# In-projection of a hybrid GLA/MLA layer: norm weights and roots applied behind the transposes, first weight loads asked for at once

## The chip, the cores and the metric

One core of one Trainium2 chip. The metric is the device time of one execution in microseconds, as the median of several runs. The profile's span is the time from the first to the last instruction of one profiled execution.

## What is computed

The kernel computes one encoder layer for 1,024 tokens of width 1,024 in float32. Only the head of the layer is touched:

```python
def _rmsnorm(x, g):
    y = x * lax.rsqrt(jnp.mean(x * x, axis=-1, keepdims=True) + EPS)
    return y * g

h = _rmsnorm(x, attn_norm)                  # (1024 tokens, 1024)
z = h @ w_in                                # (1024, 1968)
zq, zk, zv, zgate, zg, zcq, zckv, zkpe = jnp.split(z, split_pts, axis=-1)
...
gate_logit = zgate @ w_gate_up + b_gate     # decays of the gated linear attention
o_gla = _rmsnorm(gla_chunked(zq, zk, zv, ...), gla_out_norm) * silu(zg)
q  = _rmsnorm(zcq, q_a_norm) @ w_uq         # latent attention: head norms, rotary, softmax
kv = _rmsnorm(zckv, kv_a_norm) @ w_ukv
...
x = x + concat([o_gla, o_mla]) @ w_out
h = _rmsnorm(x, mlp_norm)
x = x + square(relu(h @ w_up)) @ w_down
```

The root of a token's mean square is one factor for a row of `h`, and the norm weight is one factor for a column of `h`. So `z = root(token) * ((x * weight) @ w_in)`.

## The kernel before

**Products in two parts.** A float32 product is made as three products of rounded operands: a "high" part is a rounded copy that ACT writes, a "low" part is the rest, which DVE or POOL subtracts, and `split_product` (L1741 in `mm`) adds high*high, high*low and low*high in PSUM. Every operand tile therefore passes through ACT and then DVE or POOL before TensorE can use it.

**The in-projection.** The 1,024 tokens are 8 blocks `b` of 128. The columns of `w_in` are four groups `q`: q = 0 is the 416 columns of the MLA latents together with 16 gate columns (432, `ZM`), q = 1 to 3 are 512 columns each (V, G, and Q with K). `in_project(q, b)` makes one tile of 128 tokens by one group: 8 depth tiles `k`, three products each, 24 products into PSUM bank `(8q + b) % 4`. In group q = 0 each block of x is also prepared. The order before is: ACT squares the block (`square_x`, L876), POOL makes the root (`x_rstd`, L681 and L682), DVE multiplies the block with the root and the broadcast norm weight `gain` (`norm_x`, L1214), TensorE transposes it in two halves of four (`norm_T`, L1756), ACT writes the high part (`norm_hi`, L850), DVE the low part (`norm_lo`, L1225).

**The weights.** SP loads one depth tile of weights at a time into a ring of four buffers (`raw`, `piece`, L456). For q = 0 the 16 gate columns come with a second small load for each tile (L461). A ring buffer is free when the low part that was made of it is done (`wlo_done`). ACT makes the high part (`in_high_part`), DVE the low part for q = 0 (`first_low_part`, L1342) and POOL for q >= 1 (`in_low_part`, L693). High and low parts have 10 slices: tiles 0 and 1 of the next group fit beside the 8 of the current one, and tiles 2 to 7 wait until the last block's products have freed a slice. In SP's queue, tiles 0 to 5 of q = 1 come first, then `m_uq` and `m_ukv` (the MLA up-projections), then tiles 6 and 7.

**Order within an engine.** Each engine works through a list written out by hand. POOL's list at the start is: gain load, identity, roots of blocks 0 to 7 with four small loads among them, constants (`causal`, `freq`, `ones`), four loads (`gqk` twice, `gn`, `wgate`), and then, for each block of each group, the low parts of the next group at b = 0 (tiles 0 and 1) and b = 7 (tiles 2 to 7), and the roots of the MLA latents (`c_rs`) at step `START[b] - 1`, the first at s = 5. DVE scales the latents with that root in step s = 6 (`LATENTS`), and TensorE transposes them at the end of step s = 7 (`LATENTS_T`, L1827), before the first product of q = 1.

**After the first tile of q = 1** DVE copies it out (`tile_out(8)`, L1262) and then runs `rotary_angles`. ACT waits for the angles, makes sine and cosine, and then copies the first heads out of PSUM; TensorE waits for these copies in step s = 9.

## Time and profile before

| | |
|---|---|
| median of 3 runs | 1200.38 us (1198.56 to 1200.74) |
| the profiled execution | 1200.04 us |
| its span | 1198.3 us |
| mean granted TensorE clock | 0.991 |
| busy: PE, DVE, ACT, POOL | 1160.1, 780.2, 473.7, 481.4 us |
| DMA | 158.41 MB, mean 132 GB/s |

The profiled execution lasts 1.7 us longer than its span; the rest is start and end around the first and last instruction. Times within the profile are microseconds from the span's start. In a timeline, each row gives the start and the duration; rows of several instructions of the same kind are merged, with their count. A note in brackets tells how long the engine had been idle and what released it.

### The profile page before, as it was taken

To read this page: it belongs to the slowest core of one execution; us is meant where nothing else is said; L and a number is where in the kernel's file an instruction comes from. 1 tells how busy PE (TensorE), PEld (TensorE's weight loads), DVE (VectorE), ACT (ScalarE), POOL (GpSimd) and SP (SyncE) were. 2 spreads that over 40 slices of the span, in tenths; PEclk is the share of its full clock that TensorE was granted. 3 is DMA by queue.
4 is the path that set the end of the run, shared out by engine and by line. 5 is a ranking of instruction groups with operands and counts; after the bars stand their busy time and mean duration, and the time that the engine had idled before them with its cause. 6 is when DMAs were issued, how large, how long until landed. Compare 5 with 4: busy or idle time off the path is not lost.

```text
span 1198.3 us, 15216 instructions
## 1 busy us (share of the span) xinstructions
PE 1160.1 (97%) x5586; PEld 944.4 (79%) x5586; DVE 780.2 (65%) x1012; ACT 473.7 (40%) x907; POOL 481.4 (40%) x365
## 2 busy tenths in 40 slices
PE   6999999989999999999999999999998999999998
PEld 5967677768878788887788888888876888888887
DVE  5454866535656665137668557865787888888963
ACT  5344534215545555125612233323424334443441
POOL 2442545210000114305844444445435556555652
PEclk9999999999999999999999999999998999999999
DMA  7331342264111103421354342331559785356642
GB/s 239 90 98 62 109 121 87 71 180 172 27 28 43 38 1 114 151 88 71 93 171 141 134 147 94 125 126 62 202 179 357 263 282 192 113 186 210 212 123 88
DMA packets 97353, 158.41 MB, mean 132 GB/s; under 512 B 9024, under 2 KB 38736, under 8 KB 97280
## 3 DMA queue, kind: packets, MB, share of 16 engines
q1 hardware_dynamic: 95728, 152.53, 38.6%
q10 hardware_dynamic: 1008, 3.67, 0.8%
q0 software_dynamic: 544, 1.24, 0.5%
q8 instruction: 45, 0.74, 0.3%
q14 instruction: 28, 0.23, 0.1%
HBM read 115.46 MB, written 41.94 MB: 131 GB/s over the span
## 4 chain that ended last, share of the span: by engine, by line
PE 84%; DVE 8%; issue 3%; ACT 2%; DMA 2%; POOL 1%; SPq 1%; ACTq 0%; DVEq 0%; POOLq 0%
PE ps L1741 79%; PE ps L1961 3%; DVE t_all L1515 1%; DVE g_cum L1305 1%; DVE t_new L1515 1%; PE ps L1756 1%; PE ps L1813 1%; DVE dr_lo L1515 1%; POOL wi_lo L693 1%; DMA gain<-in_attn_norm_dram 1%; DMA up_raw<-in_w_up_dram 1%; DMA r_raw<-in_w_down_dram 1%; ACT q_stage L850 0%; PE ps L1898 0%; DVE a_lo L1515 0%
## 5 line engine op out<-in xcount | busy, mean ns | idle before, releaser
L1741 PE MATMUL ps<-dr_hi,dl_hi 128*128 128x512 f32 x448 | 175.5, 392 | 4.1 <-DVE dr_lo L1515 4.1
L1741 PE MATMUL ps<-dr_hi,dl_lo 128*128 128x512 f32 x448 | 175.3, 391 | 0.0
L1741 PE MATMUL ps<-dr_lo,dl_hi 128*128 128x512 f32 x448 | 175.3, 391 | 0.0
L814 POOL TENSOR_TENSOR ua_lo<-up_raw,ua_hi 128x1024 fp32r<-128x1024 f32 x46 | 116.7, 2539 | 118.1 <-ACT ua_hi L850 118.1
L836 POOL TENSOR_TENSOR dl_lo<-l_raw,dl_hi 128x512 fp32r<-128x512 f32 x64 | 101.6, 1613 | 74.5 <-ACT dl_hi L850 74.0
L1741 PE MATMUL ps<-wi_hi,a_hi 128*128 128x512 f32 (+1 forms) x256 | 105.1, 411 | 3.5 <-POOL wi_lo L693 2.1
L1741 PEld LDWEIGHTS ps<-dr_hi,dl_hi 128*128 128x128 f32 x448 | 84.8, 189 | 22.9 <-issue 3.3
L1741 PE MATMUL ps<-a_hi,ua_hi 128*128 128x512 f32 x256 | 99.9, 390 | 2.0 <-ACT u_two L850 1.8
L836 POOL TENSOR_TENSOR dl_lo<-s_all,dl_hi 128x512 fp32r<-128x512 f32 x48 | 74.7, 1574 | 63.5 <-ACT dl_hi L850 62.6
L1741 PE MATMUL ps<-a_hi,ua_lo 128*128 128x512 f32 x256 | 99.6, 389 | 0.0
L1741 PE MATMUL ps<-a_lo,ua_hi 128*128 128x512 f32 x256 | 99.6, 389 | 0.0
L1741 PE MATMUL ps<-wi_hi,a_lo 128*128 128x512 f32 (+1 forms) x256 | 99.3, 388 | 0.0
L1741 PE MATMUL ps<-wi_lo,a_hi 128*128 128x512 f32 (+1 forms) x256 | 99.2, 388 | 0.0
L1741 PEld LDWEIGHTS ps<-dr_lo,dl_hi 128*128 128x128 f32 x448 | 84.7, 189 | 17.7
L1741 PEld LDWEIGHTS ps<-dr_hi,dl_lo 128*128 128x128 f32 x448 | 84.7, 189 | 17.6
L850 ACT ACTIVATE ua_hi<-up_raw 128x1024 fp32r<-128x1024 f32 x48 | 50.5, 1057 | 87.1 <-PE ps L1741 78.7
L1515 DVE TENSOR_TENSOR dr_lo<-r_raw,dr_hi 128x512 fp32r<-128x512 f32 x64 | 72.5, 1132 | 16.8 <-ACT dr_hi L850 16.7
L1741 PE MATMUL ps<-m_kT,m_qT 96*128 96x512 f32 (+3 forms) x192 | 77.2, 512 | 4.0 <-ACT m_p L1040 4.0
L1741 PE MATMUL ps<-tx_hi,ua_hi 128*128 128x512 f32 x192 | 75.5, 393 | 2.3 <-DVE u_three L1515 2.3
L1741 PE MATMUL ps<-tx_lo,ua_hi 128*128 128x512 f32 x192 | 75.4, 393 | 0.0
L1741 PE MATMUL ps<-tx_hi,ua_lo 128*128 128x512 f32 x192 | 75.2, 392 | 0.0
L850 ACT ACTIVATE dl_hi<-l_raw 128x512 fp32r<-128x512 f32 x64 | 39.8, 622 | 85.3 <-PE ps L1741 83.9
(221 smaller groups left out, 2470.7 us busy)
## 6 DMA issues: line engine op xcount, KB each, us to landing
r_raw<-in_w_down_dram SPq DMA_DIRECT2D x144, 256.0 KB, 3.5
hidden<-stage SPq DMA_DIRECT2D x72, 256.0 KB, 2.0
up_raw<-in_w_up_dram SPq DMA_DIRECT2D x16, 1024.0 KB, 5.6
l_raw<-hidden SPq DMA_DIRECT2D x64, 256.0 KB, 3.4
raw<-in_w_in_dram SPq DMA_DIRECT2D x24, 256.0 KB, 3.0
z_gla<-z_stage SPq DMA_DIRECT2D x16, 256.0 KB, 2.1
raw<-in_w_out_dram SPq DMA_DIRECT2D x16, 256.0 KB, 5.9
xs<-in_x_dram SPq DMA_DIRECT2D x8, 512.0 KB, 8.7
```

The costliest lines, as they stand in the source:

```text
L693: pool.tensor_tensor(wi_lo[:, n % SLICES, 0:width], raw[:, k % RING, 0:width], wi_hi[:, n % SLICES, 0:width].bitcast(F32), ALU.subtract).t ...
L814: pool.tensor_tensor(ua_lo[n % UP_RING][:, :, :], up_source(g, product), ua_hi[n % UP_RING][:, :, :].bitcast(F32), ALU.subtract).then_inc( ...
L836: pool.tensor_tensor(slot(dl_lo, t), left_source(t), slot(dl_hi, t).bitcast(F32), ALU.subtract).then_inc(dllo_done, 1)
L850: return act.activation(dst, src, ACT.Copy, scale=scale)
L1305: last = dve.tensor_tensor_scan(g_cum[:, t, blk], ones[:, :], g_log[:, t, blk], 0.0, ALU.mult, ALU.add)
L1515: return dve.tensor_tensor(out_, in0, in1, op)
L1741: return pe.matmul(dst, lhsT, rhs, start=start, stop=stop, skip_group_check=onto)
L1756: last = pe.transpose(bank4(4 + j)[:, i, :], src[:, (4 * j + i) * P:(4 * j + i + 1) * P], ident[:, :])
L1813: last = pe.transpose(bank4(4 + i // 4, DQK)[:, i % 4, :], m_qk[:, b % 2, i, :], ident[:, :])
L1961: last = pe.transpose(bank4(4 + c // 4)[:, c % 4, :], m_p[:, i % 2, c * P:(c + 1) * P], ident[:, :])
```

## The change

Blocks of x are transposed as they come from memory. The norm weight is loaded as eight rows of 128 (`gain_row`), transposed on TensorE, and copied to a column for each depth tile (`gain_col`). ACT's high part and DVE's low part of the transposed x are now made for each depth tile apart, with that column as factor, so four instructions of 128 columns stand in the place of one of 512. The root of the token is applied where a result tile is copied out of PSUM: copies become products with `rstd`; for the G group it goes into the scale of the tanh and the factor 0.5 (`half_rstd`).

For q = 0 all eight weight tiles have buffers (`raw_late` for tiles 4 to 7), and the 16 gate columns of all tiles come in one load (`raw_gate`). SP asks for the gain rows, block 0, the gate columns, the eight tiles and blocks 1 to 7 without waiting; ACT no longer issues loads of x. ACT squares block b + 1 after it has made that block's high parts, where it used to square block b + 2 before the high parts of block b + 1. TensorE multiplies the identity with itself nine times around the first transposes (`warm_up`). The first block's products start when half of its depth tiles are there. The load of the MLP's norm weight moves from POOL to SP. POOL's wait for the eight normed blocks ahead of its four loads goes.

```diff
 # SP
+            sp.dma_start(gain_row[:, :], attn_norm[0].rearrange("(k p) -> k p", p=P)).then_inc(gain_in, 16)
             sp.dma_start(x0[:, 0, :], x_d[0]).then_inc(x_in[0], 16)
+            sp.dma_start(raw_gate[:, :, :], w_in_d[:, :, C_GATE:C_GATE + GR].rearrange("k p n -> p k n")).then_inc(raw_in[0], 16)
             for k in range(KT):
                 in_piece(0, k)
+            for b in range(1, NB):
+                sp.dma_start(x0[:, b, :], x_d[b]).then_inc(x_in[b], 16)
...
+            sp.wait_ge(omT_ready, MH)
+            sp.dma_start(gain[:, :], mlp_norm[0].partition_broadcast(P)).then_inc(gain_in, 16)
 # POOL
-            pool.dma_start(gain[:, :], attn_norm[0].partition_broadcast(P)).then_inc(gain_in, 16)
...
-            pool.wait_ge(xn_ready, NB)
             pool.dma_start(gqk[:, 0, :], q_head_norm[0].partition_broadcast(P)).then_inc(phase_in, 16)
...
-            pool.wait_ge(omT_ready, MH)
-            pool.dma_start(gain[:, :], mlp_norm[0].partition_broadcast(P)).then_inc(gain_in, 16)
 # ACT
+            def x_hi(b, j):
+
+                act.wait_ge(xT_ready, 2 * b + j + 1)
+                for i in range(4):
+                    k = 4 * j + i
+                    last = copy(a_block(a_hi, k, b), bank4(4 + j)[:, i, :], gain_col[:, k:k + 1])
+                last.then_inc(ahi_done, 1)
...
+            act.wait_ge(const_ready, IDENT)
+            copy(m_rden[:, 0:1], ident[:, 0:1])
+            act.wait_ge(gain_ready, 1)
+            x_hi(0, 0)
+            act.wait_ge(raw_in[0], 32)
+            copy(wi_hi[:, 0:KT, MLA_W:ZM], raw_gate[:, :, :])
+            for k in range(2):
+                in_high_part(0, k)
+            x_hi(0, 1)
+            for k in range(2, KT):
+                in_high_part(0, k)
             x_square(0)
...
             for b in range(NB):
-                if b + 4 < NB:
-                    x_load(b + 4)
-                if b + 2 < NB:
-                    x_square(b + 2)
                 if b + 1 < NB:
-                    norm_hi(0, b + 1)
+                    for j in range(2):
+                        x_hi(b + 1, j)
+                    x_square(b + 1)
 # DVE
-            def norm_lo(r, b):
...
+            def x_lo(b, j):
+                dve.wait_ge(ahi_done, 2 * b + j + 1)
+                for i in range(4):
+                    k = 4 * j + i
+                    last = stt(a_block(a_lo, k, b), bank4(4 + j)[:, i, :], gain_col[:, k:k + 1],
+                               a_block(a_hi, k, b).bitcast(F32), ALU.mult, ALU.subtract)
+                last.then_inc(alo_done, 1)
...
                 if q == 0:
-                    dve.tensor_copy(zm[:, b, :], tile[:, 0:ZM]).then_inc(z_out, 1)
+                    dve.wait_ge(rstd_ready, b + 1)
+                    dve.tensor_scalar(zm[:, b, :], tile[:, 0:ZM], root, None, ALU.mult).then_inc(z_out, 1)
                 elif q == 1:
-                    dve.tensor_copy(z_stage[:, n % 2, :], tile).then_inc(z_out, 1)
+                    if b == 0:
+                        dve.tensor_scalar(half_rstd[:, :], rstd[:, 0, :], 0.5, None, ALU.mult)
+                    dve.tensor_scalar(z_stage[:, n % 2, :], tile, root, None, ALU.mult).then_inc(z_out, 1)
...
 # TensorE
+            def warm_up(n):
+
+                for _ in range(n):
+                    mm(ps[:, 2, 0:P], ident[:, :], ident[:, :], True, True)
...
                 for k in range(KT):
+                    if n == 0 and k % 4 == 0:
+                        pe.wait_ge(alo_done, k // 4 + 1)
...
+            pe.wait_ge(const_ready, IDENT)
+            warm_up(3)
+            pe.wait_ge(gain_in, 16)
+            pe.transpose(ps[:, 3, 0:KT], gain_row[:, :], ident[0:KT, 0:KT]).then_inc(gainT_ready, 1)
+            warm_up(2)
+            x_T(0)
+            warm_up(4)
             for b in range(NB):
                 if 1 <= b < NB - 1:
-                    norm_T(0, b + 1, x0[:, b + 1, :])
-                pe.wait_ge(alo_done, 2 * b + 2)
-                in_project(0, b, (lambda: norm_T(0, 1, x0[:, 1, :])) if b == 0 else None)
+                    x_T(b + 1)
+                if b:
+                    pe.wait_ge(alo_done, 2 * b + 2)
+                in_project(0, b, (lambda: x_T(1)) if b == 0 else None)
```

## Rows read from the trace of the kernel before

**Rows 1.** The profile's page, part 1: TensorE busy, share of the span, instructions.

```profile
PE 1160.1 (97%) x5586; PEld 944.4 (79%) x5586; DVE 780.2 (65%) x1012; ACT 473.7 (40%) x907; POOL 481.4 (40%) x365
```

**Rows 2.** Chain in order of time, 0 to 230 us: start, us, what.

```profile
1.29 6.86 DMA gain<-in_attn_norm_dram
...
9.61 1.95 PE ps L1756 x8
...
12.96 4.69 PE ps L1741 x12
...
19.30 2.35 PE ps L1741 x12
```

**Rows 3.** Timeline, all engines, start of the span: start us, us, engine, line, operation.

```profile
0.80 0.39 SPq L467 DMA_DIRECT2D x<-in_x_dram  x1
...
22.28 0.44 PE L1741 MATMUL ps<-wi_hi,a_hi 128*128 128x432 f32 x1
```

**Rows 4.** Tile x, 0 to 60 us: its loads, from issue to landing.

```profile
DMA to landing us min/median/max: 3.5/4.6/6.6
```

**Rows 5.** Windows: PE, PEld, DVE, ACT, POOL busy; PEclk, DMA share, GB/s.

```profile
3.00:6.00 3.00, 0.00 (x0) 0.00 (x0) 0.00 (x0) 0.41 (x1) 0.00 (x0) 1.00 1.02 406
6.00:9.00 3.00, 0.00 (x0) 0.00 (x0) 0.82 (x1) 1.40 (x4) 0.75 (x2) 1.00 1.01 339
```

**Rows 6.** Groups by form, ACT, 0 to 260 us: busy us, mean ns, idle before.

```profile
L850 ACT ACTIVATE a_hi<-ps 128x512 fp32r<-128x512 f32 x16 | 8.9, 596 | 17.8 <-PE ps L1756 17.8
...
L876 ACT ACTIVATE ps<-x 128x1024 f32<-128x1024 f32 x8 | 8.3, 1031 | 4.1 <-DMA x<-in_x_dram 3.8 <-issue 0.4
...
L850 ACT ACTIVATE m_cT<-ps,ga 128x128 f32<-128x128 f32 x24 | 7.0, 360 | 2.1 <-PE ps L1827 2.1
```

**Rows 7.** Groups by form, DVE, 0 to 260 us.

```profile
L1225 DVE TENSOR_TENSOR a_lo<-ps,a_hi 128x512 fp32r<-128x512 f32 x16 | 10.4, 684 | 0.5 <-ACT a_hi L850 0.5
...
L1342 DVE TENSOR_TENSOR wi_lo<-raw,wi_hi 128x432 fp32r<-128x432 f32 x8 | 4.3, 601 | 0.0
...
L1326 DVE TENSOR_SCALAR g_log<-ps,bg 128x512 f32<-128x512 f32 x4 | 3.0, 750 | 0.3
```

**Rows 8.** Timeline of ACT, 38 to 82 us.

```profile
39.82 1.04 ACT L876 ACTIVATE ps<-x 128x1024 f32<-128x1024 f32 x1
...
50.02 1.09 ACT L850 ACTIVATE a_hi<-ps 128x512 fp32r<-128x512 f32 x2 [3.66 <-PE ps L1756]
```

**Rows 9.** Timeline of POOL, 38 to 82 us; [idle before <- what ended it].

```profile
46.09 0.63 POOL L726 DMA_DIRECT2D gqk<-in_q_head_norm_dram  x1 [2.90 <-DVE x L1214]
...
48.32 2.54 POOL L693 TENSOR_TENSOR wi_lo<-raw,wi_hi 128x512 fp32r<-128x512 f32 x2
50.95 0.19 POOL L681 TENSOR_SCALAR c_rs<-c_ss 128x2 f32<-128x2 f32 x1
51.22 0.72 POOL L682 TENSOR_TENSOR c_rs<-c_rs,minus_half 128x2 f32<-128x2 f32 x1
56.51 7.54 POOL L693 TENSOR_TENSOR wi_lo<-raw,wi_hi 128x512 fp32r<-128x512 f32 x6 [4.57 <-ACT wi_hi L850]
```

**Rows 10.** Timeline of DVE, 38 to 82 us.

```profile
65.66 0.69 DVE L1262 COPY z_stage<-ps 128x512 f32<-128x512 f32 x1 [5.20 <-PE ps L1741]
```

**Rows 11.** Timeline of SP's DMA issues, 38 to 82 us.

```profile
51.96 0.86 SPq L516 DMA_DIRECT2D m_uq<-in_w_uq_dram  x1
...
57.84 11.01 SPq L456 DMA_DIRECT2D raw<-in_w_in_dram  x8
```

**Rows 12.** DMA issues, 0 to 60 us: KB each, median us to landing.

```profile
m_ukv<-in_w_ukv_dram SPq DMA_DIRECT2D x1, 512.0 KB, 6.3
```

**Rows 13.** Timeline of PE, 65 to 80 us.

```profile
77.22 0.52 PE L1827 MATMUL ps<-ident,zm 128*128 128x128 f32 x3 [1.82 <-ACT v_stage L850]
```

**Rows 14.** Timeline of SP's DMA issues, 462 to 530 us.

```profile
485.85 4.07 SPq L456 DMA_DIRECT2D raw<-in_w_out_dram  x4
```

**Rows 15.** Timeline of DVE, 462 to 530 us.

```profile
525.77 1.28 DVE L1214 SCALAR_TENSOR_TENSOR xn<-xs,rstd,gain 128x1024 f32<-128x1024 f32 x1 [2.20 <-POOL rstd L682]
```

More of the change, by code:

```diff
@@ L229, in layer @@
         h_rs = small("h_rs", [P, 2 * MH])
+        gain_row = small("gain_row", [KT, P])
+        gain_col = small("gain_col", [P, KT])
+        half_rstd = small("half_rstd", [P, NB])
         m_nm = small("m_nm", [P, 2])
@@ L283, in layer @@
         x2_stored = [sem(f"x2_stored{n}") for n in range(NB // 2)]
-        up_in = [sem(f"up_in{n}") for n in range(4)]
+        weights_in = [sem(f"weights_in{n}") for n in range(4)]
         sums_ready, uhi_done, ulo_done, part_ready = sem("sums_ready"), sem("uhi_done"), sem("ulo_done"), sem("part_ready")
@@ L296, in layer, with raw_tile, raw_landed @@
         block = ctx.enter_context(nc.Block())
[L301 to L304 removed]
+        IDENT, FREQ, ONES = 1, 2, 3
+        def raw_tile(q, k):
+            return raw_late[:, k - RING, :] if q == 0 and k >= RING else raw[:, k % RING, :]
+        def raw_landed(q, k):
+            if q == 0:
+                return (weights_in[k - RING], 16) if k >= RING else (raw_in[k], 32 if k == 0 else 16)
+            return raw_in[k % RING], 16 * (2 * (q - 1) + k // RING + 2 + (k % RING == 0))
         Q_UP = IN_GROUPS + OUT_GROUPS
@@ L452, in piece @@
             def piece(q, k, src):
-                if not (isinstance(q, int) and q == 0 and k < RING):
+                if q == 1 and k < RING:
+                    sp.wait_ge(wlo_done, k + 1)
+                elif q:
                     sp.wait_ge(wlo_done, KT * q + k - RING + 1)
-                sp.dma_start(raw[:, k % RING, 0:src.shape[-1]], src).then_inc(raw_in[k % RING], 16)
+                sp.dma_start(raw_tile(q, k)[:, 0:src.shape[-1]], src).then_inc(raw_landed(q, k)[0], 16)
             def in_piece(q, k):
@@ L721, in _ @@
                 last = pool.memset(freq[:, i:i + 1], float(ROPE_BASE ** (-2.0 * i / ROPE)))
-            last.then_inc(freq_ready, 1)
-            pool.memset(ones[:, :], 1.0).then_inc(ones_ready, 1)
-            pool.wait_ge(xn_ready, NB)
+            last.then_inc(const_ready, 1)
+            pool.memset(ones[:, :], 1.0).then_inc(const_ready, 1)
             pool.dma_start(gqk[:, 0, :], q_head_norm[0].partition_broadcast(P)).then_inc(phase_in, 16)
@@ L877, in square_x @@
                                accum_out=ssq[:, r, b:b + 1]).then_inc(ssq_ready, 1)
-            def norm_hi(r, b):
-                for j in range(2):
-                    n = 2 * (NB * r + b) + j
-                    act.wait_ge(xT_ready, n + 1)
-                    copy(a_block(a_hi, slice(4 * j, 4 * j + 4), b), bank4(4 + j)).then_inc(ahi_done, 1)
-            def x_load(b):
-                act.dma_start(x0[:, b, :], x_d[b]).then_inc(x_in[b], 16)
+            def x_hi(b, j):
[4 more added lines that the diff above has]
+                last.then_inc(ahi_done, 1)
             def x_square(b):
@@ L988, in _ @@
                             act.wait_ge(z_out, NB * q + b)
-                        act.activation(tanh_g[:, :], ps[:, b % 4, :], ACT.Tanh, scale=0.5).then_inc(tanh_ready, 1)
+                        act.wait_ge(z_out, NB + 1)
+                        act.activation(tanh_g[:, :], ps[:, b % 4, :], ACT.Tanh, scale=half_rstd[:, b:b + 1]).then_inc(tanh_ready, 1)
                     if q + 1 < IN_GROUPS and b in (0, NB - 1):
@@ L1214, in stt, with norm_x @@
                 return dve.scalar_tensor_tensor(out=out_, in0=in0, scalar=scalar, in1=in1, op0=op0, op1=op1)
-            def norm_x(r, b, src, dst):
-                dve.wait_ge(rstd_ready, NB * r + b + 1)
-                stt(dst, src[:, b, :], rstd[:, r, b:b + 1], gain[:, :], ALU.mult, ALU.mult).then_inc(xn_ready, 1)
-            def norm_lo(r, b):
-                for j in range(2):
-                    n = 2 * (NB * r + b) + j
-                    four = slice(4 * j, 4 * j + 4)
-                    dve.wait_ge(ahi_done, n + 1)
-                    dve.tensor_tensor(a_block(a_lo, four, b), bank4(4 + j),
-                                      a_block(a_hi, four, b).bitcast(F32), ALU.subtract).then_inc(alo_done, 1)
+            def norm_x(b, src, dst):
+                dve.wait_ge(rstd_ready, NB + b + 1)
+                stt(dst, src[:, b, :], rstd[:, 1, b:b + 1], gain[:, :], ALU.mult, ALU.mult).then_inc(xn_ready, 1)
+            def x_lo(b, j):
[5 more added lines that the diff above has]
+                last.then_inc(alo_done, 1)
             def rotary_angles():
                 dve.wait_ge(consts_in, 64)
-                dve.wait_ge(freq_ready, 1)
+                dve.wait_ge(const_ready, FREQ)
                 step(dve.tensor_copy(rk[:, :, 0], places[:, :]))
@@ L1255, in tile_out @@
                 tile = ps[:, s % 4, :]
+                root = rstd[:, 0, b:b + 1]
                 n = s - NB
@@ L1268, in tile_out @@
                     g4 = z_stage[:, n % 2, :].rearrange("p (h v) -> p h v", h=GH)
-                    stt(g4, g4, 0.5, gn[:, :].unsqueeze(1).broadcast_to([P, GH, GDV]), ALU.mult, ALU.mult).then_inc(z_out, 1)
+                    stt(g4, g4, half_rstd[:, b:b + 1], gn[:, :].unsqueeze(1).broadcast_to([P, GH, GDV]), ALU.mult, ALU.mult).then_inc(z_out, 1)
                 else:
                     dve.wait_ge(cum_ready, GT)
-                    dve.tensor_copy(zqk[:, b, :], tile).then_inc(z_out, 1)
+                    dve.tensor_scalar(zqk[:, b, :], tile, root, None, ALU.mult).then_inc(z_out, 1)
             def head_norms(b):
```

79 lines of the change are left out of this document (34 added, 45 removed).

## The prediction

> **What bounds the kernel now.** I read the page first, then the chain in order of time over the in-projection, then the timelines of each engine around the two places that the chain shows, then the groups by form for prices. TensorE is busy for 97% of the span [rows 1], so only its idle or slow stretches can be won. The chain shows one such place: for the first 9.6 us TensorE does nothing, because the chain runs through the 512 KB load of `gain`, which takes 6.86 us from 1.29, and the norm product behind it [rows 2]. The products begin at 12.96. Twelve of 432 columns take 4.69 us there, 0.39 each, while twelve from 19.30 take 2.35, 0.20 each [rows 2]: the lower and the upper level of the clock (1.2 and 2.4 GHz), although the column of the granted clock says 1.00 throughout [rows 5]. The second block's products begin at 22.28 [rows 3]. The second place is the change from the first group of columns (q = 0) to the second (q = 1). POOL makes the low parts of the new weights there in 7.54 us for six [rows 9], and the group's first tile is read by DVE at 65.66 [rows 10]. Everything until about 77 hangs on that read: the rotary angles, ACT's sines, ACT's copies, and the transposes at 77.22, for which TensorE has waited 1.82 us [rows 13]. So I measure the change by two marks: the start of block 1 (22.28) and DVE's read of the first q = 1 tile (65.66). Behind the second mark I let all move as one piece.
>
> **The front, removed and added.** The gain load, the root and the norm product go from in front of the first transposes. They now wait for x0 and for 4 KB of gain rows. x0 is SP's second issue, about 0.4 behind its old place at 0.80 [rows 3]. A load of x took 3.5 to 6.6 us to land, median 4.6 [rows 4], the first one beside two other loads of 512 KB. I take 3.8, so x0 lands at 5.0 (bounds 4.7 and 7.8). Four transposes at the lower level take half of 1.95 [rows 2]: 6.1 with the handoff. ACT's single pass of 512 columns (0.596) becomes four of 128 with a column of factors, 0.360 each, whose nearest row is `m_cT` [rows 6]. Two `a_hi` passes take 1.09 [rows 8], so neighbours overlap by 0.1: four cost 1.14, and `x_hi(0,0)` ends at 7.2. A quarter of 0.596 and the full 0.360 are the bounds of a pass. DVE's four products of 128 columns stand in for 0.684 [rows 7]; between a quarter of that (0.17) and ACT's 0.36 I take 0.25, so 8.3. The low parts of the gate columns (0.25) and of tile 0 (0.601 [rows 7]) follow: the first product at 9.2, against 12.96.
>
> The weights are no later than this. x0, the gate columns and tile 0 are 0.8 MB, 2 us at 406 GB/s [rows 5], and land near 7. The gate columns are now one load of 1,024 runs of 64 bytes in front of all weights. Before, eight small loads carried them, four of these by 9 us, in which time the rate fell from 406 to 339 GB/s [rows 5]. If those four cost all of that difference it is 0.5 us, so 0 to 1.0 us for the eight; I take 0.5, which lies beside the transposes. The Trainium skill (DMA: Bandwidth & Descriptors, Specifications) wants at least 512 bytes a transfer for line rate, which speaks against putting these first. It names no price, and the rows show at most 1.0 us.
>
> Then DVE sets the pace. Tile 1's low part ends at 9.8. `x_lo(0,1)` needs ACT's two weight copies and four passes and ends near 10.8. Six low parts of at most 0.601 end by 14.4. ACT squares x0 (1.03 [rows 6] and its read-out, 1.2) after its last weight copy and only then makes `x_hi(1)`, eight passes in 2.1: near 16.1. DVE follows by 17.2, the second half of block 2's transposes needs it, and block 1 starts at 17.8: 4.5 earlier. That is with the upper level reached by about 11. At 0.39 a product until 15 it is 18.5, 3.8 earlier. I take 4.0 and, with the late end of x0's landing, 2.6 to 4.5. The nine products on the identity cost nothing: TensorE has no other work before 9. The Trainium skill (TensorE: Matmul & The Clock Gate, Part 1) says that the engine starts at the low rate and that activity releases it. By it the identity products would bring the full 4.5; the trace agrees that the level rises after unbroken work, between 12.96 and 19.30.
>
> Blocks 1 to 6 stay with TensorE: 22.28 to the passes for block 7 at 50.02 [rows 3, 8] leaves about 5.6 a block, and ACT now needs 2.1 + 1.2, DVE 2.0 + 0.6. **Front: -4.0.**
>
> **What is moved, on POOL.** The squares used to run two blocks ahead: the last began at 39.82 [rows 8], and POOL, which has the roots before its constants in its queue, was through both by 43.19 (46.09 less the wait of 2.90 [rows 9]), 3.37 later. Now the last square stands behind the passes for block 7. Those begin at 50.02 - 4.0 = 46.0 and take 2.1: square at 48.1, constants done at 51.5. The four loads that POOL issues take 2.2 (46.09 to 48.32): 53.7. Two low parts to 56.3 (48.32 to 50.95), the root of the latents to 57.3 (50.95 to 51.94), six low parts, 7.54, to 64.9 [all rows 9], three products 0.7 and a handoff: DVE's mark at 65.65. Before it was 65.66 with POOL idle for 4.57 of the time [rows 9]. The whole front gain is gone: **+4.0** (3.1 to 4.8 with the bounds of ACT's pass). Behind the latents' root DVE waits too (`zm` products at 57.3, then the tile of block 7), and TensorE has the latents' transposes behind that before its first q = 1 product; both are over before POOL's sixth low part.
>
> **The loads that wait for POOL.** Weight tiles 4 and 5 of q = 1 are asked for after POOL's first and second low part. Behind them SP issues `m_uq` and `m_ukv`, 1.25 MB, and then tiles 6 and 7. The second low part ended at 50.86, and `m_ukv`, issued at 52.8, landed 6.3 later [rows 9, 11, 12], at 59.1: 8.3. Tile 6 was issued at 57.84 [rows 11], almost free of them. Now the second low part ends at 56.3, `m_uq` follows, and tile 6 is issued at 58.6 behind both. At 406 GB/s the 1.8 MB from tile 5 to tile 6 and a start-up are through by 63.3; by the old 8.3 they are through by 65.2. ACT's copy adds 0.6; POOL could have begun at 62.3. So POOL waits 0 (if tile 6 does not queue), 1.6 or 3.5. I take **+1.5**, since these loads now stand back to back, as in the rows of the front.
>
> **Scaling at the results.** Copies out of PSUM become products with a column. `g_log` shows 0.750 where a plain two-operand pass has 0.684 [rows 7]; the small product for `half_rstd` comes once ahead of the rotary angles. On the path these are 0.1 to 0.5: **+0.3**. The zm tile of 432 columns lies beside 4.7 us of products.
>
> **The second gain load** goes to SP behind the last weight tiles, which were issued by 489.9 [rows 14], and is wanted at 525.77 [rows 15]. Even the 6.86 us of the first one fit five times; POOL's lost wait frees only low parts that wait for ACT. Nothing.
>
> **Sum:** -4.0 + 4.0 + 1.5 + 0.3 = +1.8 on the profiled execution of 1200.04 (span 1198.3 and 1.7 around it). That is 1201.8; the median is 0.34 above that execution, so I say 1202.0. By the clock rule of the skill the sum would be +1.3.
>
> **The rivals.**
> *Tiles 6 and 7 at the old pace of the loads* (0.20). The two MLA loads take 8.3 us again. The third term is 3.5, the sum +3.8: 1203.8. It decides from 2.1 us of waiting. For it: that is what the trace measured. Against: POOL's own small loads lay beside them then, and the pace of TensorE wasn't asked for.
> *The front doesn't come* (0.08). If the small runs or x0 hold the first product back to 12, only 1.2 are won, and POOL takes its 4.0: +4.6, 1204.6. The rate of 339 speaks little for it.
> *The clock falls again* (0.07). While POOL sets the pace, TensorE works 0.7 of every 1.26 us. At the lower level three products take 1.4, so the pace is lost and about 2 us of the following head products with it: +3.8, 1203.8. The Trainium skill (TensorE: Matmul & The Clock Gate, Part 1) has the level fall when the engine idles; the trace shows no such fall and no such stretch.
> *The lag of POOL is covered* (0.15). If the 1.82 us wait at 77.22 and the gaps in POOL's queue take up more than 2.7 of it, the front gain stays. With all covered: -4.0 + 0.3, so 1196.4. For it: the trace has TensorE idle there. Against: that wait hangs on the same tile.
>
> **How the numbers follow.** The forecast itself has 0.50, its own range 1199.6 to 1202.8. A measurement here tells no less than 0.2%, 2.4 us. Beyond +2.4 lie the first three rivals, 0.35; below -2.4 the last, 0.15. The range 1197.6 to 1205.0 leaves out most of the covered case and the upper ends of the slow ones.
>
> **What would show it.** Right: first product near 9.2, block 1 near 18; the square of block 7 after its `a_hi` passes; POOL with no idle time between that square and the sixth low part; TensorE idle before and among the first q = 1 products; DVE's mark at 66 to 68. Wrong: DVE's mark at 62 (then it is about 1196.5), or TensorE starting after 12.

## The result: slower by half a per cent

The changed kernel takes 1206.85 us (median of 15 runs, 1200.54 to 1209.7), the kernel before 1200.21 (15 runs on the same chip, 1198.06 to 1203.73): a ratio of 1.0052, 95% interval 1.0042 to 1.0062, so 6.6 us where +1.8 was forecast. The profiled execution took 1206.98 us. The page of the changed kernel, parts 1 and 2 (beside [rows 1]):

```profile
span 1205.2 us, 15348 instructions
...
PE 1168.8 (97%) x5605; PEld 949.5 (79%) x5605; DVE 782.8 (65%) x1055; ACT 482.2 (40%) x957; POOL 480.3 (40%) x363
...
PEclk9998999999999999999999999999998999999999
```

The span is 6.9 longer, and TensorE is "busy" for 8.7 more. Of its 19 more instructions 18 are the nine identity products, which take 4.8 us at the front (1.65, 1.22 and 1.92 in its timeline), where it was idle before. The rest of the 8.7 is the old work, done more slowly. The digit 8 in the fourth slice (90 to 120 us) says the same, and the mean granted clock is 0.986, against 0.991.

**The front came as forecast.** The chain of the changed kernel, 0 to 30 us (beside [rows 2]):

```profile
1.25 3.67 DMA x<-in_x_dram
4.97 1.13 PE ps L1782 x4
...
6.18 1.15 ACT a_hi L869 x4
7.36 1.13 DVE a_lo L1233 x4
```

x0 is there at 4.97, the high parts end at 7.3, and the timeline of its PE shows the first product at 9.33 and block 1 at 16.99, where it was 22.28 [rows 3]:

```profile
9.33 0.43 PE L1767 MATMUL ps<-wi_hi,a_hi 128*128 128x432 f32 x1 [0.69 <-DVE wi_lo L1369]
...
9.80 0.35 PE L1767 MATMUL ps<-wi_hi,a_lo 128*128 128x432 f32 x1
9.99 0.35 PE L1767 MATMUL ps<-wi_hi,a_hi 128*128 128x432 f32 x1
...
16.99 0.44 PE L1767 MATMUL ps<-wi_hi,a_hi 128*128 128x432 f32 x1
```

The step from 9.80 to 9.99 is 0.19: the upper level (2.4 GHz) from the first product on. The front wins 5.3, not 4.0.

**Then POOL is late, as forecast, and what stands behind it is not.** ACT, then POOL, of the changed kernel, 38 to 82 us (beside [rows 8, 9]):

```profile
44.72 2.18 ACT L869 ACTIVATE a_hi<-ps,gain_col 128x128 fp32r<-128x128 f32 x8 [1.53 <-PE ps L1782]
46.73 1.08 ACT L895 ACTIVATE ps<-x 128x1024 f32<-128x1024 f32 x1
...
62.25 1.30 ACT L869 ACTIVATE wi_hi<-raw 128x512 fp32r<-128x512 f32 x2 [3.27 <-DMA raw<-in_w_in_dram]
```

```profile
52.33 2.53 POOL L716 TENSOR_TENSOR wi_lo<-raw,wi_hi 128x512 fp32r<-128x512 f32 x2
...
55.92 5.00 POOL L716 TENSOR_TENSOR wi_lo<-raw,wi_hi 128x512 fp32r<-128x512 f32 x4
62.95 2.53 POOL L716 TENSOR_TENSOR wi_lo<-raw,wi_hi 128x512 fp32r<-128x512 f32 x2 [2.03 <-ACT wi_hi L869]
```

The last square stands behind the `a_hi` passes for block 7, and POOL runs without a pause from its root at 48.02 through the low part of tile 5. Tile 6, issued at 57.21 behind `m_uq` and `m_ukv`, lands 5 us later, and POOL waits 2.03 for it (forecast 1.5). DVE in the changed kernel, the second mark last (beside [rows 10]):

```profile
55.98 1.36 DVE L1343 TENSOR_SCALAR zm<-zm,c_rs 128x256 f32<-128x256 f32 x1 [5.45 <-POOL c_rs L705]
57.26 1.28 DVE L1344 TENSOR_SCALAR zm<-zm,c_rs 128x128 f32<-128x128 f32 x1
...
67.04 0.74 DVE L1286 TENSOR_SCALAR z_stage<-ps,rstd 128x512 f32<-128x512 f32 x1
```

The first of these rows in the kernel before, where POOL was idle beside it:

```profile
55.67 0.34 DVE L1319 TENSOR_SCALAR zm<-zm,c_rs 128x256 f32<-128x256 f32 x1
```

The two products with the latents' root take 2.6 us and not 0.6, because POOL began its next low part at 55.92, just ahead of them. They take 0.35 and 0.28 in e2, e5, e6, e7, e8 and e10 too, where no low part runs beside them, and about 1.36 and 1.28 in e1, e3, e4, e9 and e11, where one has just begun. So 2.0 of TensorE's idle time of 4.07 behind them is DVE standing beside POOL, and only the rest is POOL's late root. The forecast has no term for it.

67.04 against 65.66: +1.4 at the mark, where the forecast had +1.5 (+1.8 with the scaling). The number holds, but not by the path that was forecast. POOL's sixth low part ended at 65.48, where the forecast had 64.9 and 1.5 of waiting, 66.4. Where POOL's last tile sets the mark, DVE reads 1.1 us behind it (1.12 in e1, 1.13 in e2 and e9), which would be 66.6. Here TensorE had no idle time between 59.15 and the mark; it made the tile's first products on the lower level and was 0.4 later than that. So part of the agreement is luck.

**Behind the mark came the rest.** The starts of TensorE's transposes of the latents `zm` (L1827 before, L1860 after, one set for each block) are good milestones, since they recur in each group. Five of the eight:

| | before | after | lag |
|---|---|---|---|
| first behind the mark | 77.22 | 78.66 | +1.4 |
| next | 106.89 | 109.94 | +3.1 |
| next but one | 125.11 | 128.16 | +3.1 |
| then | 152.72 | 158.37 | +5.7 |
| last of the in-projection | 212.34 | 218.08 | +5.7 |
| span | 1198.3 | 1205.2 | +6.9 |

Two stretches carry 4.2 of the 5.5: 1.6 between the first two rows and 2.6 between the third and the fourth. The windows of the changed kernel (columns as in [rows 5]; the last three are the granted clock, the DMA share and GB/s):

```profile
57.00:60.00 3.00, 1.41 (x5) 1.31 (x6) 2.12 (x3) 0.65 (x2) 3.00 (x4) 0.50 1.00 384
60.00:63.00 3.00, 3.00 (x8) 2.32 (x8) 0.00 (x0) 0.72 (x2) 0.97 (x2) 0.50 1.01 381
...
97.00:100.00 3.00, 3.00 (x6) 0.71 (x4) 1.71 (x3) 0.00 (x0) 0.00 (x0) 0.61 0.22 82
100.00:103.00 3.00, 3.00 (x8) 2.42 (x8) 2.41 (x2) 0.00 (x0) 0.32 (x2) 0.50 0.00 0
...
149.00:152.00 3.00, 3.00 (x8) 2.32 (x8) 2.92 (x5) 2.97 (x3) 1.33 (x2) 0.50 0.80 259
```

The same windows of the kernel before, which the prediction did not show:

```profile
57.00:60.00 3.00, 3.00 (x19) 2.85 (x18) 0.15 (x1) 1.20 (x3) 3.00 (x3) 1.00 0.55 184
...
97.00:100.00 3.00, 3.00 (x9) 2.01 (x7) 2.83 (x3) 0.00 (x0) 0.00 (x0) 0.60 0.00 0
100.00:103.00 3.00, 3.00 (x12) 2.44 (x11) 0.00 (x0) 0.00 (x0) 2.89 (x2) 0.83 0.00 0
```

In the windows at 0.50 TensorE is on the lower level (1.2 GHz): eight instructions begun or running in 3 us, 0.43 apart for 512 columns, where they stand 0.23 apart on the upper level. Summed over windows of 1 us through the whole span, the changed kernel is low for 34.1 us and the kernel before for 20.5. Half of low time is lost work, so 13.6 more cost up to 6.8. (Outside the stretch discussed here, one of 3.4 at 596 us is new and one at 271 is 3.4 shorter than its counterpart at 264.) Over all runs the same: 1206.85 at a median clock of 0.987 is 1191.2 at full clock, 1200.21 at 0.991 is 1189.4, so 1.8 of the 6.6 is left for everything that isn't the clock (each clock is rounded to 0.001, 1.2 us, so this 1.8 is rough).

What stood ahead of the three low stretches of the in-projection that are new or longer (timeline of PE, changed kernel):

```profile
58.59 0.90 PE L1860 MATMUL ps<-ident,zm 128*128 128x128 f32 x3 [4.07 <-DVE zm L1344]
...
95.23 4.83 PE L1767 MATMUL ps<-zgateT,wgate 16*128 16x512 f32 x8
...
148.23 0.50 PE L1767 MATMUL ps<-wi_hi,a_hi 128*128 128x512 f32 x1 [2.09 <-POOL wi_lo L716]
```

At 58.59 it is an idle time of 4.07 behind POOL's late root and DVE's slowed products. The Trainium skill (TensorE: Matmul & The Clock Gate, Part 1) has the level fall when the engine idles; this trace agrees: 1.00 before the idle time, 0.50 behind it. At 95.23 it is no idle time: the gate logits (four products of 16 rows, eight instructions) fill it. In the kernel before they take 3.69 from 93.79 and the level falls at their end, at 97.5; here it falls at 97.5 too, 2.3 into them, which is why they take 4.83. At 148.23 it is POOL again, late because ACT waited for the last weight tile of the next group. That tile's load took longer. DMA of the changed kernel, 141 to 147 us, then of the kernel before, 138 to 144 us, in which queues are listed with packets, MB and share of 16 engines:

```profile
q8 instruction: 1, 0.02, 2.1%
...
raw<-in_w_in_dram SPq DMA_DIRECT2D x1, 256.0 KB, 4.3
```

```profile
q1 hardware_dynamic: 409, 0.74, 38.2%
...
raw<-in_w_in_dram SPq DMA_DIRECT2D x1, 256.0 KB, 3.0
```

In the changed kernel one packet of 16 KB on q8, a load of instructions, lies on the tile's load. Before, the nearest ones lay at 110 and 144, beside it. They return every 24 to 34 us in the kernel before. An open question at this point was whether that packet is the cause or a bystander.

### The profile page after: what moved, and what is told of

Read it like the earlier page. It is cut to its first block, busy times and chain, and to the rows that moved or that the text cites. A ratio compares the mean times of both kernels' runs of the same rounds, so it can differ in the third digit from the quotient of the medians.

```text
span 1205.2 us, 15348 instructions
## 1 busy us (share of the span) xinstructions
PE 1168.8 (97%) x5605; PEld 949.5 (79%) x5605; DVE 782.8 (65%) x1055; ACT 482.2 (40%) x957; POOL 480.3 (40%) x363
## 4 chain that ended last, share of the span: by engine, by line
PE 84%; DVE 7%; issue 3%; DMA 2%; ACT 2%; POOL 2%; SPq 0%; ACTq 0%; DVEq 0%
PE ps L1767 78%; PE ps L2000 3%; POOL wi_lo L716 1%; DVE t_all L1541 1%; DMA r_raw<-in_w_down_dram 1%; PE ps L1846 1%; DVE t_new L1541 1%; DVE dr_lo L1541 1%; DMA up_raw<-in_w_up_dram 1%; PE ps L1782 1%; ACT a_hi L869 0%; DMA raw<-in_w_in_dram 0%; PE ps L1937 0%; DVE a_lo L1541 0%; DVE stage L1541 0%
## 5 line engine op out<-in xcount | busy, mean ns | idle before, releaser
L1767 PEld LDWEIGHTS ps<-dr_hi,dl_lo 128*128 128x128 f32 x448 | 84.7, 189 | 17.8
```

The source lines that it names most:

```text
L1767: return pe.matmul(dst, lhsT, rhs, start=start, stop=stop, skip_group_check=onto)
```

## The experiments

Theory A: POOL's lateness (the square and the constants in its queue) makes the idle time at 54 to 58, and through it the late mark and the low level there. Theory B: what comes behind the mark is the clock and the late tile, not the work that the change added. Its rival, C: the products with the root and the single passes cost more than they look. All are compared with runs of the kernel before on the same chip. "Mark" is DVE's read of the first q = 1 tile in the one profiled execution.

| run | median us (runs) | before | ratio, 95% interval | mark |
|---|---|---|---|---|
| changed kernel | 1206.85 (15) | 1200.21 | 1.0052, 1.0042 to 1.0062 | 67.04 |
| e1, POOL's constants early | 1203.36 (12) | 1200.40 | 1.0030, 1.0019 to 1.0041 | 62.52 |
| e2, squares ahead | 1199.89 (12) | 1200.40 | 1.0001, 0.9987 to 1.0016 | 61.09 |
| e3, no identity products | 1204.05 (12) | 1200.40 | 1.0033, 1.0019 to 1.0048 | 69.35 |
| e4, the wait filled | 1203.63 (12) | 1200.40 | 1.0025, 1.0012 to 1.0039 | 68.03 |
| e5, squares and more products | 1195.42 (10) | 1200.77 | 0.9965, 0.9950 to 0.9979 | 60.83 |
| e6, squares, latent loads last | 1197.93 (12) | 1200.77 | 0.9984, 0.9965 to 1.0003 | 60.53 |
| e7, squares, logits apart | 1199.94 (12) | 1200.77 | 0.9989, 0.9974 to 1.0004 | 61.21 |
| e8, before with identity products | 1201.57 (12) | 1200.77 | 1.0002, 0.9986 to 1.0018 | 67.26 |
| e9, changed with ten products | 1202.28 (12) | 1200.52 | 1.0016, 1.0002 to 1.0031 | 67.10 |
| e10, e5 and e6 together | 1195.29 (7) | 1200.52 | 0.9960, 0.9942 to 0.9978 | 60.23 |
| e11, changed, 15 products first | 1208.32 (9) | 1200.52 | 1.0063, 1.0044 to 1.0083 | 70.28 |

### e1 and e2: POOL on time, in two ways

e1 changes POOL's queue, in the changed kernel: the constants and the four small loads go ahead of the roots of blocks 3 to 7.

```diff
-            for b in range(3, NB):
-                x_rstd(b)
...
             pool.dma_start(wgate[:, :], w_gate_up[0]).then_inc(phase_in, 16)
+            for b in range(3, NB):
+                x_rstd(b)
```

> The changed kernel, but POOL builds its constants and issues its four loads after the root of block 2 and not after that of block 7. Theory (POOL's late queue makes TensorE idle between the two column groups, and the idle stretch costs the clock too): the 4.1 us wait before the latents' transposes goes, the level stays high at 57 to 64 us, DVE's read of the first q = 1 tile comes at 61 to 62 instead of 67.0, and the time falls by 5 to 7 us against the changed kernel, to about 1195 to 1200 beside 1200.2 before. Rival (the loads of the weights hold this place, not POOL): the read stays at 65 or later and the time within 2 us of the changed kernel.

e2 changes ACT's queue instead: squares two blocks ahead, as in the kernel before.

```diff
-                    x_square(b + 1)
+                    if b == 0:
+                        x_square(1)
+                    if b + 2 < NB:
+                        x_square(b + 2)
```

> The changed kernel, but ACT squares each block from block 2 on one block earlier, so POOL's last root comes about 5.6 us earlier while POOL's own list is untouched. Theory (it is the lateness of the last square that pushes POOL's list): nearly the same result as with POOL's constants moved, the read of the first q = 1 tile at 61 to 63. Rival (something else in POOL's list or in the order of loads): no change of that mark.

The marks come at 62.52 and 61.09, 4.5 and 5.9 earlier than in the changed kernel. DVE in e1, PE in e1, then DVE in e2:

```profile
62.52 0.74 DVE L1287 TENSOR_SCALAR z_stage<-ps,rstd 128x512 f32<-128x512 f32 x1
```

```profile
55.03 0.55 PE L1861 MATMUL ps<-ident,zm 128*128 128x128 f32 x3 [0.58 <-DVE zm L1345]
```

```profile
61.09 0.75 DVE L1289 TENSOR_SCALAR z_stage<-ps,rstd 128x512 f32<-128x512 f32 x1
```

The idle time of 4.07 is 0.58 or gone, and so is the low stretch at 57 to 63. Theory A is shown, by two edits on different engines. The totals fall by 3.5 and 7.0; for e1 I had expected 5 to 7. What is left of the idle time in e1 is DVE's two products, which still stand beside POOL there (1.37 and 1.30). But against the kernel before e2 is level, although its mark is 4.6 earlier: the low stretch behind the logits and the late tile (5.0 us to land in e1, a q8 packet on it at 139 and 136) are still there in both, and cost what the front won.

### e3: without the identity products

The changed kernel without `warm_up(3)`, `warm_up(2)` and `warm_up(4)`.

> The changed kernel without the nine products of the identity with itself. If the level of the clock rises by activity, the first block's products run at the lower level (0.36 to 0.39 each for 432 columns instead of 0.20), block 1 starts at 18 to 19 instead of 17.0, and the time rises by 1 to 2 us unless POOL's list hides it (then the read of the first q = 1 tile moves by the same amount). Rival: the level at that point does not depend on the identity products, and block 1 starts at 17.0.

The first product starts at 9.42, at the lower level, 0.36 apart (PE, 0 to 20 us), and block 1 at 18.78, 1.8 later than with them:

```profile
9.92 0.56 PE L1767 MATMUL ps<-wi_lo,a_hi 128*128 128x432 f32 x1
10.28 0.56 PE L1767 MATMUL ps<-wi_hi,a_lo 128*128 128x432 f32 x1
...
18.78 0.44 PE L1767 MATMUL ps<-wi_hi,a_hi 128*128 128x432 f32 x1
```

So the nine products bring 1.8 at the front and 2.3 at the mark. Yet the kernel without them is 2.8 faster by the medians, where 1 to 2 us more were expected. In the stretch with the weight tile (125 to 152 in the kernel before) it needs 27.5 against 30.2 with them, and no q8 packet lies on the tile: it falls at 149. This was the first sign that the number of TensorE's instructions before a place decides where the loads of instructions fall.

### e4: the idle time filled

18 identity products, which need the last square and nothing else, at the end of `in_project(0, 7)`, ahead of the wait for the latents' root.

```diff
+                if b == NB - 1:
+                    pe.wait_ge(ssq_ready, NB)
+                    for _ in range(18):
+                        mm(ps[:, 6, 0:P], ident[:, :], ident[:, :], True, True)
```

> The changed kernel, with 18 products of the identity with itself where TensorE waits 4.1 us ahead of the latents' transposes; POOL stays as late. It tells POOL's delay from the price of the clock. If the idle stretch makes the level fall: no low level at 57 to 64, the read of the first q = 1 tile 1 to 1.5 us earlier (65.5 to 66, where POOL's low parts alone put it). Rival (the level falls for another reason): low level and mark as in the changed kernel.

The clock stays up (1.00 at 57 to 63), but the mark is 68.03 and not the 65.5 to 66 that I wrote down. PE, then windows, of e4:

```profile
55.32 4.18 PE L1767 MATMUL ps<-ident 128*128 128x128 f32 x36
...
65.69 0.50 PE L1767 MATMUL ps<-wi_hi,a_hi 128*128 128x512 f32 x1 [1.42 <-POOL wi_lo L716]
```

```profile
69.00:72.00 3.00, 3.00 (x7) 1.71 (x6) 3.00 (x6) 0.00 (x0) 2.66 (x3) 0.63 0.31 91
```

POOL's late tiles set the mark, so a faster TensorE only waits for them (1.42), and the level falls 10 us later, at 67 to 72. Against the changed kernel the mark isn't really later: in this execution `a_hi` of block 7 already began at 45.68, against 44.72, ahead of the edit, and POOL waited 2.39 for tile 6 instead of 2.03; 0.3 of these 1.3 us came back, with the clock up. So one profiled mark can be read to about 1 us. The median is 3.2 below the changed kernel's, but the 36 instructions also move the q8 packets (127 and 160, off the tile), so not all of this is the filled wait.

### e5: squares ahead and more identity products

e2, with six instead of four products behind the first transposes, and ten more at the end of step s = 9.

```diff
-            warm_up(4)
+            warm_up(6)
...
                     in_project(q, b)
+                    if NB * q + b == GATE_T:
+                        pe.wait_ge(z_out, NB - 1)
+                        warm_up(10)
                     behind(NB * q + b)
```

> The version with the squares ahead, plus 12 products of the identity with itself: two at the front and ten in the 2.3 us wait ahead of the second latents' transposes (near 71). They change nothing but how many instructions TensorE has run by 136 us. Theory: in the changed kernel and in the two versions that move POOL's or ACT's work, a 16 KB load of TensorE's instructions falls on weight tile 7 of the third group (it lands in 4.3 to 5.0 us instead of 3.0), TensorE then idles 3 us and the level falls for 3.4 us. With about 48 more TensorE instructions ahead that load comes some 5 us earlier: tile 7 lands in about 3 us, no low level near 144, and the time falls by 2 to 4 us, to 1196 to 1198. Rival (the lateness of tile 7 is unrelated to the instruction load): no change there, 1199 to 1201.

1195.42 us, 0.35% below the kernel before and 11.4 us below the changed kernel's median (10.4 by the two ratios), with more TensorE instructions than either. That is also below the 1196 to 1198 that I expected. Its windows:

```profile
90.00:93.00 3.00, 3.00 (x8) 1.03 (x6) 2.75 (x6) 0.00 (x0) 0.00 (x0) 1.00 0.23 87
93.00:96.00 3.00, 3.00 (x14) 2.45 (x14) 2.41 (x2) 0.00 (x0) 0.41 (x2) 1.00 0.02 5
```

The logits lie at 89 to 93 here, in the same row of eight, and the level doesn't fall behind them. The q8 packets lie at 122 and 156, off the tile, and ACT waits 1.20 for it. Nothing is low before 261 us.

### e6, e7 and e8: three sizes

e6 is e2 with SP's issue of `m_uq` and `m_ukv` moved behind tiles 6 and 7.

> The version with the squares ahead, with the two loads of the latents' up-projections (1.25 MB) asked for behind weight tiles 6 and 7 and not ahead of them. My third term says that these tiles queue behind them: tile 6 lands in about 2.7 us instead of 4.3, DVE's read of the first q = 1 tile comes 1 to 1.5 us earlier than 61.1, and the time falls by about as much, unless the up-projections now come late (their landing must be before 61). Rival: no queueing, the mark stays at 61.1.

The mark comes at 60.53, 0.56 earlier than in e2, where I wrote 1 to 1.5: with POOL on time its wait for ACT's copy of tiles 6 and 7 was 1.34 in e2, and only part of that was the queue. e7 is e2 with each gate-logit product set behind one of the depth steps k = 0 to 3 of the in-projection step, so that they no longer follow each other.

> The version with the squares ahead, with the gate logits' 16-row products not in one run of 3.7 us but one behind each of the first four depth tiles of the next block. If these products, though they fill TensorE's time, let the level fall (low for 6.8 us at 92 to 100 in this version), the low stretch goes and the time falls by about 3 us, to about 1197. Rival (the level there falls for another reason): the low stretch stays.

The expected gain isn't there. PE, then a window, of e7:

```profile
98.07 2.07 PE L1770 MATMUL ps<-zgateT,wgate 16*128 16x512 f32 x2
```

```profile
97.00:100.00 3.00, 3.00 (x5) 0.88 (x5) 0.75 (x1) 0.00 (x0) 0.00 (x0) 0.57 0.00 0
```

The four pairs still lie within 6 us of each other (they begin at 91.96, 93.90, 95.85 and 98.07), and the level falls just ahead of the last, which takes 2.07 against 1.12 for the others. This profiled execution (1204.12) is the slowest of e7's twelve. e8 is the kernel before with 12 identity products ahead of its first transposes and 4 behind.

> The kernel before, with 16 products of the identity with itself around the first transposes and nothing else of the change: one part alone. If they raise the level before 12.96, the first block's twelve products run at 0.20 each instead of 0.39, block 1 starts about 2 us earlier than 22.28, and the time falls by up to 2 us to about 1198.5; where POOL's low parts of the second group hold the pace, less of it. Rival (no gain at all): 1200.4, block 1 at 22.3.

The products start at 13.01 on the upper level, 0.20 apart, and then TensorE is too early: it waits 2.53 for DVE's low parts, block 1 starts at 22.47 instead of 22.28, and the level falls. PE, then a window, of e8:

```profile
21.37 1.44 PE L1756 MATMUL ps<-ident,x 128*128 128x128 f32 x8 [2.53 <-DVE a_lo L1225]
```

```profile
22.00:25.00 3.00, 3.00 (x11) 2.82 (x12) 2.63 (x4) 2.74 (x5) 0.58 (x2) 0.52 0.96 306
```

The 1.0002 (0.9986 to 1.0018) shows no gain from a raised clock alone where the next operand is late.

### e9, e10 and e11: the price of the clock and of the tile, on the changed kernel

e9 is the changed kernel with only the ten products of e5 at the end of step s = 9; POOL stays late.

> The changed kernel with ten identity products at the end of step s = 9, ahead of the gate column transposes, and nothing else; POOL stays late (DVE's mark near 67, low level 57 to 64). Theory (what is lost behind the mark is the granted clock and a weight tile held up by an instruction load, whose place depends on the number of TensorE instructions before it): the instruction load leaves the time around 142, the last weight tile of the next group lands in 3.0 us, the interval from the transposes near 128 to those near 157 falls from 30.2 to 28 or less, and with TensorE unbroken at 80 to 95 the low stretch at 97 to 105 goes; 1202 to 1204 against 1206.85. Rival (the loss is work of the change, in products with the root and the like): both intervals stay, 1207 to 1209. Other rival: the instruction load moves and the low stretch at 97 stays: 1204 to 1205.

The mark is the old one, 67.10, and the time falls by 4.6. ACT's wait for the late tile in the changed kernel, then in e9, then a window of e9:

```profile
145.34 0.63 ACT L869 ACTIVATE wi_hi<-raw 128x512 fp32r<-128x512 f32 x1 [2.27 <-DMA raw<-in_w_in_dram]
```

```profile
142.74 0.63 ACT L869 ACTIVATE wi_hi<-raw 128x512 fp32r<-128x512 f32 x1 [1.12 <-DMA raw<-in_w_in_dram]
```

```profile
147.00:150.00 3.00, 3.00 (x15) 2.49 (x14) 2.94 (x4) 2.97 (x4) 1.33 (x1) 1.00 0.98 311
```

The q8 packets moved to 103 and 130, the tile lands in 3.0 us, TensorE stays on the upper level there, and the interval 128 to 158 (30.2) becomes 28.6 (28 or less was expected). The low stretch behind the logits is 3.4 us now, at 99 to 103, instead of 6.8: the interval from 79 to 109 is 29.7 against 31.3. Ten products that compute nothing, in the middle of the queue, take back 4.6 of 6.6. The work that the change added stayed as it is, so C can at most be the rest: theory B is shown for these 4.6 us. How they split is less firm. By the median clocks (0.990 here, 0.987 in the changed kernel) 3.7 of them are the clock, which leaves about 1 for the tile. (The level behind the idle time of 4.1, which is still there, was low for 3.4 us in e9 and 6.8 in the changed kernel; that is part of the 4.6.)

e10 joins e5 and e6.

> The best two edits together: squares ahead, the extra identity products (six after the first transposes, ten at the end of step s = 9), and the latent attention's weight loads behind tiles 6 and 7 of q = 1. If the gains add: no low stretch at 97, DVE's mark at 60.5, 1194 to 1195. Rival: the late latent loads move nothing, and the low stretches fall elsewhere: 1195 to 1198.

1195.29 us: no different from e5 within what is measured. e11 has 15 instead of 3 identity products at the very start, and nothing else.

> The changed kernel with 15 instead of 3 identity products at the very start, where TensorE waits for block 0 of x until 4.97; nothing else. The front costs nothing or up to 1 us, and DVE's mark stays at 67 to 68. Theory (the place of the instruction loads follows the number of TensorE instructions): the one at 142 falls about 3 us of work earlier, the last weight tile of the next group is on time, and the time is 1204 to 1206; if it falls on another tile, that one is late instead. Rival (the late tile has another cause): tile 7 stays at 4.3 us and the time at 1206 to 1208.

Front, mark and time (1208.32 against 1204 to 1206) all missed; the tile was on time, as expected. PE of e11, 0 to 22 us:

```profile
1.58 5.43 PE L1767 MATMUL ps<-ident 128*128 128x128 f32 x30 [1.58 <-POOL ident L726]
...
7.64 1.04 PE L1782 MATMUL ps<-ident,x 128*128 128x128 f32 x8
```

I had not multiplied: 15 float32 products stand as 30 instructions and take 5.43, so x0's transposes start 2.7 late. TensorE then idles 1.92 ahead of the first product, the lower level comes back at 12 to 16 us, and block 1 starts at 20.16, 3.2 later. The mark is 3.2 later too. But the packets now lie at 105 and 131, ACT waits 1.10 for the tile, and the interval with it is 28.6 instead of 30.2. 3.2 - 1.6 is +1.6 on 1206.85, and 1208.32 was measured; the agreement is loose, since the profiled execution of e11 (1203.83) is 4.5 below its median and has no low stretch behind the logits. So the time of e11 supports nothing here; the tile's wait is read directly. A third, independent shift of the instruction count (e3 nine fewer products, e9 ten more behind, e11 twelve more ahead) takes the packet off the tile and with it the wait. A count over the windows from 0 bears this out: when the fifth q8 packet comes, TensorE has begun 1149 to 1183 matmuls and weight loads in all thirteen kernels, although that moment lies anywhere between 122 us (e5) and 149 us (e3). In e1, e2 and e7, with a packet at 136 to 140 on the load, ACT waited 3.05 to 3.19; in e3, e4, e5, e8, e9 and e11, without one, 1.07 to 1.20. In e6 (packet at 134) it was 1.55.

**What the late tile really costs.** TensorE's idle time behind it is 2.08 or 2.09 in all five kernels that have it (changed, e1, e2, e6, e7), whether ACT waited 3.19 or 1.55. POOL and DVE show why. The changed kernel, then e6:

```profile
145.32 1.73 DVE L1303 TENSOR_TENSOR m_qk<-m_qk,h_rs 128x1536 f32<-128x1536 f32 x1
146.05 2.12 POOL L716 TENSOR_TENSOR wi_lo<-raw,wi_hi 128x512 fp32r<-128x512 f32 x1 [0.93 <-ACT wi_hi L869]
```

```profile
135.88 1.73 DVE L1305 TENSOR_TENSOR m_qk<-m_qk,h_rs 128x1536 f32<-128x1536 f32 x1
135.92 2.82 POOL L715 TENSOR_TENSOR wi_lo<-raw,wi_hi 128x512 fp32r<-128x512 f32 x1 [0.24 <-ACT wi_hi L868]
```

In both POOL's low part ends 1.12 to 1.13 us behind the end of DVE's product, whenever it began: it got nothing done while that product ran. When the tile is on time POOL begins first, and then DVE's product takes 2.77 instead of 1.73 (e9, and the kernel before with 2.78) and TensorE waits only 0.39. So a tile that is 0.4 us late (e6) costs as much as one that is 2 us late: TensorE's 1.7 us are the turn that POOL loses to DVE. A little later the same meeting, with POOL's next low part and DVE's last rotary product, goes with the whole interval between the transposes. It is 30.1 to 30.2 in the five kernels with the lost turn, 28.5 to 28.6 in e4, e5, e8, e9, e10 and e11, where that DVE product takes 1.51 to 1.54, and 27.5 to 27.6 in e3 and the kernel before, where the tile is on time and the product takes 0.42.

## Why the prediction was wrong

**First step, what bounds the kernel.** Right in its two marks, wrong in its last sentence: "Behind the second mark I let all move as one piece." This is the step that failed. At the mark the sum came out (+1.4 measured, +1.5 forecast), in part by luck, as told above. Behind it 5.5 more were lost: 1.6 between 77 and 107, 2.6 between 125 and 152, 1.2 after the in-projection. e9 takes back 4.6 of it without touching POOL, the roots or the front.

**The front, -4.0.** Right mechanism, size -5.3. Landing (3.67 taken as 3.8), transposes, ACT's and DVE's four passes (1.15 and 1.13 for 1.14 and about 1.0) and the first product (9.33 for 9.2) fit; block 1 came 0.8 before the forecast 17.8. The identity products are worth 1.8 of it (e3).

**POOL, +4.0.** Right, and +4.7 in size: the mark's +1.4 is -5.3, plus this, plus the 2.0 below. It is a difference and holds the 0.4 that the lower level cost at the mark. The last square began at 46.73, 1.4 ahead of the forecast 48.1, and POOL was ahead by as much up to the latents' root (55.94 for 57.3). e1 and e2, which shorten that wait too, move the mark by 4.5 and 5.9. What I wrote of the wait for the latents' root, "both are over before POOL's sixth low part", missed the price: DVE's two products took 2.0 us longer beside POOL, and the 4.07 us of idle TensorE put it on the lower level for 6.8 us, until 63.5.

**The loads that wait for POOL, +1.5.** POOL waited 2.03 in the changed kernel, where the forecast was 1.6 and the rival's value 3.5. That rival (0.20) fell. So did the two others: the front came, and POOL's lag was not covered, since ACT's copies behind the same tile hold the transposes at 78.66 as they did before at 77.22 (a wait of 1.95, against 1.82 [rows 13]).

**Scaling, +0.3.** Nothing in the traces speaks against it: DVE's read of the first tile takes 0.74 instead of 0.69. e9 leaves no more than 2 us for all that isn't clock or tile.

**The clock falls again (0.07).** This one came true, with a chance too low and a price too small (+2). Its place was wrong: I put it into the stretch where POOL sets the pace, and it began in the idle time ahead of that, then came back twice, in the logits and behind the late tile. The prediction's "the trace shows no such fall and no such stretch" was false of the whole trace. The kernel before already showed such stretches (97 to 103 at 0.60 and 0.83), and no row of it was read for them. That a stretch just at the edge of falling is moved by anything ahead of it is my reading; no run tests it alone. "The column of the granted clock says 1.00 throughout" was a statement on rows of the first 9 us. (One sum: 1200.04 + 1.8 + 0.34 is 1202.2 and not 1202.0, and the rivals' times leave the 0.34 out; nothing hangs on it.)

**Still open.** Why the level falls in or behind the same eight logit instructions in the changed kernel, e1, e2, e3 and e7 (6.8 us), e9 (3.4) and the kernel before (3.4), and not in e4, e5, e6, e8, e10 and e11. e7 shows that their standing in a row isn't it. Nor need these be traits of the kernels: each has one profiled execution, and the 15 runs of the changed kernel spread from a mean clock of 0.984 to 0.991, so its low stretches differ from one execution to the next. Only the medians of many runs are a firm measure of what the clock costs a kernel. Also open: the 1.2 us behind the in-projection, which is of the size by which single executions differ there.

## What to carry to other kernels

A front that is won is worth what the next queue lets through, so follow each producer (here ACT's square, then POOL's root) to the next point where another engine waits for it, and cost every idle time of TensorE that opens on the way twice: once as time, and once as half of the low stretch behind it. Where TensorE sets the pace for hundreds of microseconds, read the granted clock of the whole span in short windows before predicting, and count what stands just ahead of each low stretch. Where POOL and DVE meet, ask which begins first: here 0.4 us of lateness turned into 1.7 because the other engine got its turn. A change of a half per cent that also changes the number of instructions should be repeated with a few harmless instructions added or taken away; here ten empty products moved the time by 4.6 us.

## What the runs showed of the hardware

- One load of 16 KB of instructions (one packet on q8) on top of a 256 KB weight load went with a landing of 4.3 instead of 3.0 (changed kernel; 5.0 in e1). The fifth such packet comes when TensorE has begun 1149 to 1183 matmuls and weight loads, in all thirteen kernels.
- A POOL subtraction and a DVE instruction did not run side by side in the pairs read here: DVE's `zm` product took 1.36 beside a low part and 0.34 alone, POOL's low part took 2.82 beside a DVE product of 1.73 and ended 1.13 behind it. The one that began first kept its time.
- TensorE can be busy without a gap and the level falls all the same: 3.69 us of products of 16 rows in the kernel before, then 0.50; in the changed kernel 0.50 from 2.3 us into them.
- The granted clock reads 1.00 over the first 15 us of e3, and its first products behind it stand 0.36 apart for 432 columns, the spacing of the lower level. At the start the column can't be used; the spacing can.
- Runs of one kernel follow their mean clock: the changed kernel's lie from 1200.54 at 0.991 to 1209.7 at 0.984.
